# Sixteen-row products of a three-layer block run in pairs on two groups of TensorE's rows or columns

## The reference, cut to what matters

```
# SSD mixer: 16 heads, chunks of 128 tokens
h = x @ w_in;  ...;  dt_raw = last 16 columns of h
dt = softplus(dt_raw + dt_bias);  a = -exp(a_log)
a_cs = cumsum(dt * a, within a chunk)                      # 16 heads x 512 tokens: "decay sums"
seg = exp(where(causal, a_cs[t] - a_cs[s], -inf))          # per head and chunk
y_diag = (C B^T * seg) @ (x dt);   y_off = C @ prev_state * exp(a_cs)
# fox mixer: 16 heads
f_logit = last 16 columns of x @ w_in;  log_f = log_sigmoid(f_logit + b_f);  cum = cumsum(log_f)
scores = q k^T * scale + cum[query] - cum[key]
```

## Time and profile before

| | before |
|---|---|
| time, median of 3 runs | 2733.8 us (2732.25 to 2737.7) |
| the profiled execution: time / span | 2734.03 us / 2732.2 us |
| TensorE clock granted, mean over the span | 0.989 |
| PE busy | 2644.3 us (97%) |
| DVE, ACT, POOL busy | 1180.5, 550.8, 82.3 us |
| time step (L970), 16 records | 7.04 us from first start to last end |
| forget gate (L1191), 16 records | 7.04 us |
| decays (L1135), 32 records in 7 stretches | 3.72 us once, 1.98 us six times |

### The profile page before, as it was taken

The page is one execution under the profiler, slowest core; times in us unless marked ns, Lnnn a source line. Parts: engine busy times, 40 slices in busy tenths (PEclk is TensorE's granted clock), DMA queues, the critical chain, the costliest instruction groups (busy, mean ns, idle before and its releaser), DMA issues.

```text
span 2732.2 us, 28630 instructions
## 1 busy us (share of the span) xinstructions
PE 2644.3 (97%) x9532; PEld 1709.3 (63%) x9532; DVE 1180.5 (43%) x2154; ACT 550.8 (20%) x1168; POOL 82.3 (3%) x116
## 2 busy tenths in 40 slices
PE   7998999999999999999998999999999889999998
PEld 3444444476444447888745888847744448888657
DVE  3046564152111117647375766611500756666313
ACT  2124001021000002213222322200211432222101
POOL 0001000000000000000020000000000100000000
PEclk9999999999999999999999999999999999999999
DMA  3223221227999952222112222223222002222223
GB/s 126 77 70 139 77 77 62 77 85 259 358 335 337 336 202 91 91 93 85 62 47 69 93 85 84 92 77 123 100 78 70 0 23 93 93 92 84 85 99 124
DMA packets 89024, 317.63 MB, mean 116 GB/s; under 512 B 9536, under 2 KB 11584, under 8 KB 88928
## 3 DMA queue, kind: packets, MB, share of 16 engines
q1 hardware_dynamic: 80096, 283.33, 29.9%
q10 hardware_dynamic: 5152, 19.92, 1.8%
q0 software_dynamic: 3696, 13.31, 1.5%
HBM read 294.43 MB, written 22.02 MB: 116 GB/s over the span
## 4 chain that ended last, share of the span: by engine, by line
PE 91%; DVE 5%; ACT 2%; issue 1%; DMA 1%; DVEq 0%; ACTq 0%; POOL 0%; SPq 0%; POOLq 0%
PE bank L566 35%; PE bank L1022 26%; PE bank L836 12%; PE bank L1001 3%; PE bank L1077 2%; PE bank L654 2%; PE bank L1204 2%; ACT R L1294 2%; DVE stat L1720 1%; PE bank L1086 1%; DVE R L1735 1%; PE bank L602 1%; PE bank L676 1%; PE bank L592 1%; PE bank L1135 1%
## 5 line engine op out<-in xcount | busy, mean ns | idle before, releaser
L566 PE MATMUL bank<-arena,ring 128*128 128x256 f32 (+2 forms) x1840 | 564.2, 466 | 3.8 <-DVEq L2031 1.6
L566 PEld LDWEIGHTS bank<-arena,ring 128*128 128x128 f32 x1840 | 349.4, 190 | 213.4 <-issue 182.1
L566 PE MATMUL bank<-X,ring 128*128 128x512 f32 x912 | 398.0, 594 | 6.9 <-ACT X L1239 5.8
L836 PE MATMUL bank<-arena 128*128 128x512 f32 x768 | 336.0, 597 | 3.0 <-ACT arena L1440 1.9
L1022 PE MATMUL bank<-SQ,arena 128*128 128x256 f32 x1440 | 330.4, 379 | 0.0
L566 PEld LDWEIGHTS bank<-X,ring 128*128 128x128 f32 x912 | 173.6, 191 | 225.8 <-issue 224.8
L1022 PEld LDWEIGHTS bank<-SQ,arena 128*128 128x128 f32 x1440 | 273.6, 190 | 37.2
L836 PEld LDWEIGHTS bank<-arena 128*128 128x128 f32 x768 | 145.7, 192 | 180.6 <-issue 180.6
L1022 PE MATMUL bank<-X,ring 128*128 128x256 f32 x960 | 227.4, 379 | 0.0
L1022 PEld LDWEIGHTS bank<-X,ring 128*128 128x128 f32 x960 | 182.3, 190 | 25.6 <-issue 0.9
L1022 PE MATMUL bank<-SQ,ring 128*128 128x256 f32 x480 | 113.5, 379 | 0.9 <-DVE R L2341 0.9
(11 more groups left out here) (340 smaller groups left out, 2583.1 us busy)
## 6 DMA issues: line engine op xcount, KB each, us to landing
ring<-w_stream SPq DMA_DIRECT2D x336, 512.0 KB, 3.3
arena<-w_stream SPq DMA_DIRECT2D x192, 512.0 KB, 5.5
y_slots<-X ACTq DMA_DIRECT2D x1, 9216.0 KB, 26.2
y_slots<-arena ACTq DMA_DIRECT2D x16, 512.0 KB, 6.7
X<-x_t SPq DMA_DIRECT2D x2, 1024.0 KB, 8.5
x_tok<-arena ACTq DMA_DIRECT2D x1, 2048.0 KB, 6.6
out_t<-X SPq DMA_DIRECT2D x16, 128.0 KB, 2.3
part<-params SPq DMA_DIRECT2D x1, 824.0 KB, 11.1
```

Source lines behind the costliest of these rows:

```text
L566: mm = pe.matmul(mbank(t)[:, 0:width], w, r, start=(k == 0), stop=(k == len(rhs) - 1))
L836: mm = pe.matmul(bank[t % 4][:, :], w_, ERING[:, at:at + S], start=(k == 0), stop=(k == len(lhs) - 1))
```

## The change

1. `time_step` and the forget gate become one function, `sixteen_rows`. Products with even k add up in partitions 0 to 15 of the bank (array columns 0 to 15), those with odd k in partitions 64 to 79 (columns 64 to 79).
2. ACT therefore copies two pieces out of the bank (L1499 as before, and a plain copy of partitions 64 to 79), and DVE adds them (a 16 x 512 sum ahead of `log1p_abs`).
3. `decays` handles two heads: the even one from rows 0 to 15, the odd one from rows 64 to 79 of `SEL16` and `ACS`, so on two groups of array rows; their outputs lie in two banks, as before.
4. For this POOL loads the selector a second time (to partitions 64 to 79), and DVE copies `ACS` there after the scans. PE waits for both once, ahead of the first decays.

```
+            def sixteen_rows(name, w):
+                t = A0[name]
                 a_read(pe, t - 4)
                 for k in range(C8):
-                    mm = pe.matmul(abank(t)[0:16, :], pmat("w_dt", k, 16), X[:, k], start=(k == 0), stop=(k == C8 - 1))
+                    r = 64 * (k % 2)
+                    mm = pe.matmul(abank(t)[r:r + 16, :], pmat(w, k, 16), X[:, k], start=(k < 2), stop=(k >= C8 - 2))
                 mm.then_inc(a_full, 1)
...
-            def decays(h):
-                t = head_tile(h)
-                a_read(pe, t - 4)
-                pe.matmul(abank(t)[:, :], SEL16[0:16, h * P:(h + 1) * P], ACS[0:16, :], start=True, stop=True)\
-                    .then_inc(a_full, 1)
-            pe.wait_ge(sel_loaded, 16)
+            def decays(j):
+                for n in range(2):
+                    h, r = 2 * j + n, slice(64 * n, 64 * n + 16)
+                    t = head_tile(h)
+                    a_read(pe, t - 4)
+                    mm = pe.matmul(abank(t)[:, :], SEL16[r, h * P:(h + 1) * P], ACS[r, :], start=True, stop=True)
+                    mm.then_inc(a_full, 1)
+            pe.wait_ge(sel_loaded, 32)
+            pe.wait_ge(acs_twice, 1)
...
-                act.activation(b[0:16, 0], abank(t)[0:16, :], ACT.Identity, bias=pc(bias, 0, slice(0, 16)))\
-                    .then_inc(a_out[t % 4], 1)
+                act.activation(b[0:16, 0], abank(t)[0:16, :], ACT.Identity, bias=pc(bias, 0, slice(0, 16)))
+                act.activation(b[0:16, 5], abank(t)[64:80, :], ACT.Copy).then_inc(a_out[t % 4], 1)
...
                 a_read(dve, A0[src_tile])
+                step.inc(dve.tensor_tensor(x_, x_, b[0:16, 5], ALU.add))
+                sync()
...
                 ins.then_inc(dte, 1)
+                dve.wait_ge(dte, 1)
+                dve.tensor_copy(ACS[64:80, :], ACS[0:16, :]).then_inc(acs_twice, 1)
...
-            pool.dma_start(SEL16[0:16, :], sel16).then_inc(sel_loaded, 16)
+            for r in (0, 64):
+                pool.dma_start(SEL16[r:r + 16, :], sel16).then_inc(sel_loaded, 16)
```

More of the change, by code:

```diff
@@ L199, in build @@
             sem(n) for n in ("st_prod", "st_copy", "st_sum", "st_out", "st_weights", "st_inputs"))
-        f_e, f_ln, f_cum, f_rows, f_ones = (sem(n) for n in ("f_e", "f_ln", "f_cum", "f_rows", "f_ones"))
+        f_e, f_ln, f_cum, f_rows, f_ones, acs_twice = (
+            sem(n) for n in ("f_e", "f_ln", "f_cum", "f_rows", "f_ones", "acs_twice"))
         out_done = sem("out_done")
@@ L964, in _ @@
             token_transposes(1)
-            def time_step():
-                t = A0["dt"]
+            def sixteen_rows(name, w):
+                t = A0[name]
                 a_read(pe, t - 4)
                 for k in range(C8):
-                    mm = pe.matmul(abank(t)[0:16, :], pmat("w_dt", k, 16), X[:, k], start=(k == 0), stop=(k == C8 - 1))
+                    r = 64 * (k % 2)
+                    mm = pe.matmul(abank(t)[r:r + 16, :], pmat(w, k, 16), X[:, k], start=(k < 2), stop=(k >= C8 - 2))
                 mm.then_inc(a_full, 1)
@@ L1055, in seven_products @@
                 if stage == "s_in":
-                    time_step()
+                    sixteen_rows("dt", "w_dt")
                     for p in range(2, 22):
@@ L1129, in _ @@
                               start=True, stop=True).then_inc(a_full, 1)
-            def decays(h):
-                t = head_tile(h)
-                a_read(pe, t - 4)
-                pe.matmul(abank(t)[:, :], SEL16[0:16, h * P:(h + 1) * P], ACS[0:16, :], start=True, stop=True)\
-                    .then_inc(a_full, 1)
-            pe.wait_ge(sel_loaded, 16)
+            def decays(j):
[7 more added lines that the diff above has]
+            pe.wait_ge(acs_twice, 1)
             decays(0)
-            decays(1)
             for c in range(NT):
@@ L1145, in _ @@
                 if j < C8 - 1:
-                    decays(2 * j + 2)
-                    decays(2 * j + 3)
+                    decays(j + 1)
                     if j == 6:
@@ L1186, in _ @@
             four_by_halves(T0["fqk"], "lnf0", {(0, 0): lambda: r_stats("lnf0", 1)})
[L1188 to L1192, removed]
+            sixteen_rows("f", "w_f")
             def fqk(i):
```

## The result

| | before | changed |
|---|---|---|
| time, median (range) | 2734.78 us (2732.25 to 2737.7, 4 runs) | 2715.09 us (2714.52 to 2718.92, 4 runs) |
| ratio to before, 95% interval | | 0.9931 (0.9913 to 0.9948) |
| a later series of runs | 2734.66 us (10 runs) | 2719.19 us (2718.61 to 2720.65, 5 runs), ratio 0.9946 (0.9933 to 0.996) |
| profiled execution, time / span | 2734.03 / 2732.2 us | 2718.92 / 2717.1 us |

The change makes the kernel faster by 19.7 us, and by 15.5 us in the later series.

A forecast was written before the change was run, and what follows sets the result against it. TensorE, busy 97% of the span, was taken as the bound. Time step 3.0, forget gate 3.0, decays 3.9 and clock 1.6 sum to 11.5 us saved, giving 2722.3 us, range 2719.5 to 2728.5.

The forecast's parts named there:

- What bounds the kernel, and that savings reach the end: TensorE, busy 97% of the span, with the chain through the three touched products; what PE saves there, everything following starts earlier.
- 2n records then need n + 1 slots in place of 2n: Paired thin products and decays; a slot is one record, 0.43 us; saves 3.0, 3.0 and 3.9 us.
- A2 runs beside B1: Assumed start order for neighbouring fp32 products A and B, two records each: A's second record overlaps B's first.
- Row groups pair as column groups do: Decays: saving between 0 and 3.9 us, upper bound taken; the rival that they don't pair had chance 0.11.
- The clock behind the first decays, 1.6 us: At `sout_first`: the fall to half clock more likely absent, 1.6 us gained; rival that it falls anyway, chance 0.28.
- Falls of the clock elsewhere, "some 1.6 us either way": Later stretches where PE waits could catch or lose a clock fall through the shift in time, some 1.6 us.
- The additions are hidden: ACT's second copy, DVE's sum and `ACS` copy, POOL's load and PE's waits fall inside existing waits, cost 0.
- DVE in the SSD rounds: DVE's wait for the pair's products is used up in round one, then 0.78 us slack each; not the bound.
- The rule that a weight load overlaps products in flight only where their groups of rows differ: Time step and forget gate: by it column pairs gain nothing, sum 5.5 us in place of 11.5; the prediction rejected it.
- The rivals: Clock falls anyway 0.28, row groups don't pair 0.11, column groups don't 0.03, nothing pairs 0.04, slower by group changes 0.04.
- with row groups alone in pairs: Rival: column groups don't pair, only the decays gain; saved 3.9 us, 2729.9 us, chance 0.03.

The follow-up runs named there:

- e3: Changed kernel, but column groups alternate only after two products in the time step and four in the forget gate; median 2718.47 us, ratio 0.9935.
- e2: Changed kernel with both thin products (time step, forget gate) put back, so only the decays run in pairs; median 2722.44 us, ratio 0.9954 to before.
- e6: Changed kernel, but the first stretch of eight decay records is on one row group, later decays paired; median 2720.56 us, ratio 0.9951 to before.
- e7: Changed kernel, but only the first eight decay records are paired, the six later stretches on one row group; median 2725.18 us, ratio 0.997 to before.
- e4: Changed kernel with every product back on one group of rows or columns, all additions kept; median 2734.81 us, ratio 1.0001 to before.
- e5: Changed kernel with time step and forget gate on four column groups, four ACT copies and three DVE sums; median 2715.54 us, ratio 0.9933 to before.

## Why the prediction was right or wrong

- *What bounds the kernel, and that savings reach the end*: right. The savings are seen whole in the segment and at the forget gate.
- *"2n records then need n + 1 slots in place of 2n", with "A2 runs beside B1"*: this is the step that failed. It is n. I laid an order of starts over the row of 28 records without testing it. By n + 1 the last of them starts 14 x 0.107 = 1.50 us behind the first, by n 1.39 us; the row has 1.48, which seems to speak for n + 1. But the first eight records take 0.48 us, where four slots are 0.43, and each later stretch of four takes 0.22, two slots: the surplus is spread over the row and is no slot at its end (timeline of PE before):

```profile
1370.31 0.39 PE L1166 MATMUL bank<-R,SQ 128*64 128x128 f32 x4
1370.53 0.39 PE L1160 MATMUL bank<-R,arena 128*64 128x128 f32 x4
```

The last four records could have told as well: they span 0.39 us, one length of 0.27 and one distance of 0.11, so two slots for four records, where A2 beside B1 gives three. With n the sum of slots is 8 + 8 + 4 + 12 = 32 in place of 23, 13.7 us in place of 9.9: 3.8 us of the miss of 8.2. e3 shows why: a record passes up to three waiting ones.
- *Row groups pair as column groups do*: right, the upper bound was the value (e2).
- *The clock behind the first decays, 1.6 us*: right in place, sign and size (e2, e6, e7).
- *Falls of the clock elsewhere, "some 1.6 us either way"*: mis-sized. The later fall gives 1.85 us more, in both profiles of either kernel, and the two series of the changed kernel differ by 4.1 us between themselves. With 9.9 corrected to 13.7 and the 1.85 added, the sum is 17.2 us, between the 19.7 and 15.5 measured; 2.5 us of the first result stay without a place.
- *The additions are hidden*: right (e4), with 0.18 us of cover left on ACT, as forecast, and 0.18 behind the scans.
- *DVE in the SSD rounds*: not the bound, but later than I said. In the first two rounds it takes up a pair 2.1 and 0.25 us after PE has it, and then waits 0.35 us in two rounds, not 0.78, because PE's round shrinks by two slots (0.85) and not one; in the next two it waits 0.94:

```profile
1368.96 0.74 DVE L2431 SCALAR_TENSOR_TENSOR arena<-arena,part,bank 128x512 f32<-128x512 f32 x1
1376.90 0.74 DVE L2431 SCALAR_TENSOR_TENSOR arena<-arena,part,bank 128x512 f32<-128x512 f32 x1
1386.50 0.75 DVE L2431 SCALAR_TENSOR_TENSOR arena<-arena,part,bank 128x512 f32<-128x512 f32 x1 [0.35 <-PE bank L1170]
```

- *The rule that a weight load overlaps products in flight only where their groups of rows differ* (the Trainium skill, TensorE: Matmul & The Clock Gate, Part 3, "The mechanism"): the trace doesn't agree; two, and in e5 four, column groups with all rows in common load and multiply together.
- *The rivals*: none came. One was mis-added: with row groups alone in pairs the clock's 1.6 us belongs to the saving too, so 5.5 us and not 3.9, as the paragraph on the rule has it. With n slots and the later fall, e2 has 8.46 us of segment and 1.85 behind it.

## What to carry to other kernels

Products that use few rows or columns of the array (16 here) take about half the time when neighbours go to different groups, rows and columns alike, also for fp32 with its two records, and on four column groups about a quarter (7.04 to 1.91 us). Keep the groups alternating: runs of two fp32 products cost nothing here, runs of four did. When a row holds several records, work out the distance of the first and the last start in a short stretch before laying an order over a long one. And compare profiles over a segment between two instructions: here it repeats to 0.1 us where two medians of one kernel differ by 4.

## What was unexpected of the hardware

- PE starts a record of a free group past three waiting records of a busy one (e3: 8 slots for runs of two, 12 for runs of four; e5: 4 slots for four groups).
- The clock fell to 1.2 GHz behind 3.7 us in which PE was busy all the time, but with 16 of its 128 rows; with the rows in pairs (1.99 us) it didn't fall. With 16 of 128 columns for 7.04 us it stayed at 1.00 (PE by windows before, the forget gate):

```profile
1968.00:1975.00 7.00, 7.00 (x18) 1.00 0.00 1
```

- The falls of the clock behind the first decays, among the transposes and behind the rounds come again with about the same length in a second profile of the same program, while the time up to the time step varies by some us. A change elsewhere in the program can add a fall (e5: one more among the transposes, 0.9 us, some 250 us behind the products that changed).
